# Down product of a decoder trunk's first row part in plain fp32, and a top-k search shared out anew between two engines

## What is computed

```python
# DSA: the 256 best-scoring keys of each query row, then attention over these
_, sel = lax.top_k(score, n_sel)
# MLP, D_FF = 2816 = 22 chunks of 128 columns
g_conv, new_ffn = causal_dwconv(ffn_buf, xn2 @ W['w_gate'][i], W['conv_ffn'][i])
h = h + (jax.nn.silu(g_conv) * (xn2 @ W['w_up'][i])) @ W['w_down'][i]
```

## Time and profile before

| what | us |
|---|---|
| median of three runs | 1925.38 |
| profiled execution, its own time | 1921.14 |
| its span | 1919.5 |
| PE busy in the span | 1699.0 |
| DVE busy | 1153.1 |
| ACT busy | 748.1 |

### The profile page before, as it was taken

The page is one execution under the profiler, slowest core; times in us unless marked ns, Lnnn a source line. Parts: engine busy times, 40 slices in busy tenths (PEclk is TensorE's granted clock), DMA queues, the critical chain, the costliest instruction groups (busy, mean ns, idle before and its releaser), DMA issues.

```text
span 1919.5 us, 27805 instructions
## 1 busy us (share of the span) xinstructions
PE 1699.0 (89%) x9909; PEld 1528.4 (80%) x9909; DVE 1153.1 (60%) x2454; ACT 748.1 (39%) x1349; POOL 211.3 (11%) x356
## 2 busy tenths in 40 slices
PE   6989998987768888778999998799999999998894
PEld 5978897863557666556888898799999999997793
DVE  5456764386767876688655554455555555554544
ACT  4343443353568477723444432232222222225321
POOL 1000000121101212222633100000000000000000
PEclk9999999998867777878999999899999999999996
DMA  5321121331312222232323223112121212231002
GB/s 182 108 99 55 56 86 65 110 117 47 99 39 90 83 78 77 86 110 67 108 90 96 75 68 124 55 55 78 66 77 66 76 66 76 66 104 45 22 34 90
DMA packets 50226, 153.19 MB, mean 80 GB/s; under 512 B 9456, under 2 KB 12528, under 8 KB 50112
## 3 DMA queue, kind: packets, MB, share of 16 engines
q1 hardware_dynamic: 35248, 116.13, 17.7%
q0 software_dynamic: 14864, 35.60, 5.9%
HBM read 141.92 MB, written 9.76 MB: 79 GB/s over the span
## 4 chain that ended last, share of the span: by engine, by line
PE 55%; issue 12%; DVE 9%; ACT 5%; DMA 1%; POOLq 1%; POOL 1%; DVEq 0%; ACTq 0%
PE ps L1874 20%; PE ps L735 14%; PE ps L1975 8%; ACT act_junk L1230 3%; PE ps L1356 2%; PE ps L1396 2%; PE ps L1410 2%; PE ps L2141 1%; PE ps L1368 1%; PE ps L1422 1%; PE ps L1050 1%; DVE Pb_b L1605 1%; DVE wl L521 1%; DVE junk_b L1174 1%; DVE SC L1082 1%
## 5 line engine op out<-in xcount | busy, mean ns | idle before, releaser
L521 DVE TENSOR_TENSOR wl<-wr,wh 128x1024 fp32r<-128x1024 f32 x202 | 246.7, 1223 | 295.6 <-ACT wh L514 294.2
L514 ACT ACTIVATE wh<-wr 128x1024 fp32r<-128x1024 f32 x202 | 213.0, 1056 | 456.2 <-PE ps L1874 196.0
L1874 PE MATMUL ps<-xh_b,wh 128*128 128x336 f32 x832 | 264.7, 318 | 8.7 <-DVE xl_b L619 4.9
L1874 PE MATMUL ps<-xl_b,wh 128*128 128x336 f32 x832 | 265.1, 319 | 0.0
L1874 PE MATMUL ps<-xh_b,wl 128*128 128x336 f32 x832 | 263.4, 317 | 0.0
L735 PE MATMUL ps<-xh_a,wh 128*128 128x384 f32 x592 | 219.9, 372 | 22.7 <-DVE xl_a L619 8.4
L735 PE MATMUL ps<-xh_a,wl 128*128 128x384 f32 x592 | 217.5, 367 | 0.0
L735 PE MATMUL ps<-xl_a,wh 128*128 128x384 f32 x592 | 214.7, 363 | 0.0
L1874 PEld LDWEIGHTS ps<-xh_b,wh 128*128 128x128 f32 x832 | 157.6, 189 | 10.5 <-DVE wl L521 4.1
L1874 PEld LDWEIGHTS ps<-xh_b,wl 128*128 128x128 f32 x832 | 157.6, 189 | 0.0
L1874 PEld LDWEIGHTS ps<-xl_b,wh 128*128 128x128 f32 x832 | 157.2, 189 | 0.0
(11 more groups left out here) (365 smaller groups left out, 3432.5 us busy)
## 6 DMA issues: line engine op xcount, KB each, us to landing
wr<-in_weights SPq DMA_DIRECT2D x202, 512.0 KB, 3.5
pages<-in_d_pages POOLq DMA_DIRECT2D x128, 128.0 KB, 2.4
out_y<-TN SPq DMA_DIRECT2D x8, 528.0 KB, 2.7
pages<-in_c_pages POOLq DMA_DIRECT2D x128, 32.0 KB, 2.1
H<-in_xT SPq DMA_DIRECT2D x8, 336.0 KB, 9.3
H<-in_xT POOLq DMA_DIRECT2D x8, 336.0 KB, 5.4
H<-in_xT SPq DMA_DIRECT2D x8, 192.0 KB, 5.5
H<-in_xT POOLq DMA_DIRECT2D x8, 192.0 KB, 4.5
```

The source lines that it names most:

```text
L514: nc.scalar.activation(wh[:, slot], wr[:, slot], ACT.Copy).then_inc(w_hi, 1)
L521: nc.vector.tensor_tensor(wl[:, slot], wr[:, slot], wh[:, slot].bitcast(f32), ALU.subtract).then_inc(w_lo, 1)
L1874: last = nc.tensor.matmul(bank(first_bank + c)[:, 0:CB], w, x, start=k == 0 and t == 0, stop=k == KC - 1 and t == 2)
```

## The change

Three things:

1. The first part's down product takes the raw weights `wr` and the undivided rows `gu_a` in plain fp32, with no split of either, over four chunks at a time (five groups of four and one of two). The weights are stored a second time in the order this needs (W_DA on); each such block holds 4 chunks for 2 of the 8 outputs. A group's four blocks are used one after each of the next four chunks. `gu_a` holds eight chunks. `half_conv` is made once for all chunks, and the two zero columns of `ge_a` are set once.
2. Each mask becomes two stages, `need` (count, comparison, how many equal ones to take) and `mask` (scan and the rest); the threshold gets a stage `found`, where the reload of the scores is now issued.
3. Array 2 (768 keys) of the search moves from ACT to DVE.

```diff
-ACT_TOP = [4, 3, 2, 1]
-DVE_TOP = [5, 0]
+ACT_TOP = [4, 3, 1]
+DVE_TOP = [5, 2, 0]
...
+def add_down(g, part):
+    left = min(4, FC - 4 * g)
+    rows = 8 // left
+    ORDER.append(W_DA + 4 * g + part if left == 4 else ff_block("d", 4 * g, part))
+    SKIPPED.append(len(ORDER) - 1)
+    QUANTA.extend(("d", g, rows * part + m, left, len(ORDER) - 1) for m in range(rows))
+for f in range(FC):
+    add_chunk(f)
+    if f >= 4:
+        left = min(4, FC - f // 4 * 4)
+        for part in range(f % 4 * 4 // left, (f % 4 + 1) * 4 // left):
+            add_down(f // 4 - 1, part)
+for part in range(2):
+    add_down(QUADS - 1, part)
...
+LENGTH = [{"d": 4 * NA, "pb": CB}.get(QUANTA[n][0], NA) for n, _ in MM]
...
-            + [("mask", NTOP - 1)] + [("mask", j) for j in range(NTOP - 1)])
+            + ["found"] + [(what, j) for j in [NTOP - 1, *range(NTOP - 1)] for what in ("need", "mask")])
-    weights = [{"sign": 4, "ties": 8, "mask": 8}.get(s[0] if type(s) is tuple else s, 4) for s in stages]
+    weights = [{"sign": 4, "ties": 8, "mask": 6, "found": 2}.get(s[0] if type(s) is tuple else s, 4) for s in stages]
...
             if j == 0:
-                pe.wait_ge(w_lo, s + 1)
+                if kind == "d":
+                    pe.wait_ge(w_raw[s % 3], 16 * (s // 3 + 1))
+                else:
+                    pe.wait_ge(w_lo, split_no(s) + 1)
...
                 if kind == "d":
-                    pe.wait_ge(a_lo, 2 * f + 2)
+                    pe.wait_ge(a_mul, 4 * f + count)
...
             if kind == "d":
                 cols = slice(0, NA)
-                w, x = three(t, s % 3, (ah_a[:, (2 * f + k) % 3], al_a[:, (2 * f + k) % 3]), 4 * k + c % 4)
+                rows = 8 // count
+                w, x = wr[:, s % 3, rows * j + c % rows], gate_up_a(4 * f + j)
...
-                nc.scalar.activation(ah_a[:, f % 3], gv_a[:, f % 2, 0:NA], ACT.Copy).then_inc(a_hi, 1)
...
-                nc.vector.tensor_tensor(al_a[:, f % 3], gv_a[:, f % 2, 0:NA], ah_a[:, f % 3].bitcast(f32), ALU.subtract).then_inc(a_lo, 1)
...
-            nc.vector.tensor_tensor(v, v, bank(6 + n % 2)[:, 0:NA], ALU.mult).then_inc(a_mul, 1)
+            nc.vector.tensor_tensor(gate_up_a(f), v, bank(6 + n % 2)[:, 0:NA], ALU.mult).then_inc(a_mul, 1)
...
-            nc.vector.memset(e[:, 0:2], 0.0)
-            link(nc.vector.tensor_scalar(w, p_("conv_ffn")[:, 3 * f:3 * f + 3], 0.5, None, ALU.mult))
...
-        SEARCHED_AT = [4 * n + p for (n, p), s in B_STAGE_AT.items() if s == ("mask", NTOP - 1)][0]
+        SEARCHED_AT = [4 * n + p for (n, p), s in B_STAGE_AT.items() if s == "found"][0]
```

More of the change, by code:

```diff
@@ L172, with spread @@
 assert 4 * (IDX_STEP + 6) == 4 * SIDX_STEP
-def spread(total, places):
-    weight = sum(w for _, w in places)
-    out, done = {}, 0
+def spread(first, last, places):
+    weight, total = sum(w for _, w in places), sum(LENGTH[first:last])
+    out, done, n, length = {}, 0, first, 0
     for place, w in places:
         done += w
-        out[place] = round(total * done / weight)
+        while n < last and length + LENGTH[n] / 2 <= total * done / weight:
+            length += LENGTH[n]
+            n += 1
+        out[place] = n
+    out[places[-1][0]] = last
     return out
 MM = [(n, j) for n, q in enumerate(QUANTA) for j in range(q[3]) if q[0] != "pa"]
+LENGTH = [{"d": 4 * NA, "pb": CB}.get(QUANTA[n][0], NA) for n, _ in MM]
 N_PB, N_OUT = 2 * NZ * 24, KC * 24
@@ L190 @@
 ISSUED = {}
[L191 to L194, removed]
+ISSUED |= spread(0, N_PB, [(p, 1) for p in range(0, 4 * PROJ_END)])
+ISSUED |= spread(N_PB, N_PB + N_OUT, [(p, 1) for p in range(4 * PROJ_END, NORM_AT - 4)])
+ISSUED |= spread(N_PB + N_OUT, len(MM), [(p, 1.0 if p < 4 * DSA_B else 1.2) for p in range(FFN_AT, NPOS)])
 for p in range(NPOS):
@@ L215, in limit @@
     return min([NPOS - 1] + [START[a] for a in (n,) if a in START])
-FREE_AT, HI_AT, LO_AT, CONV_AT, TANH_AT, MUL_AT, AH_AT, AL_AT = ({} for _ in range(8))
+FREE_AT, HI_AT, LO_AT, CONV_AT, TANH_AT, MUL_AT = ({} for _ in range(6))
 MUL_FIRST = {}
@@ L243 @@
         MUL_FIRST[f] = at > tanh_at
-        at = put(AH_AT, min(at + 1, limit(down)), f)
-        put(AL_AT, min(at + 1, limit(down)), f)
 for s in range(NZ + 2, NFIRST):
+    if s in SKIPPED:
+        continue
     first = limit(FIRST_Q[s])
@@ L700, in build, with split_no, gate_up_a @@
         LAST_A_UNIT = unit(A_END)
+        def split_no(s):
+            return s - sum(a < s for a in SKIPPED) if type(s) is int else s - len(SKIPPED)
+        def gate_up_a(f):
+            return gu_a[:, f % 8] if f % 8 < 6 else gu_rest_a[:, f % 8 - 6]
         def freed(n):
@@ L1253, in thresholds, with need @@
                 dve.wait_ge(self.searched, 1)
-            def mask(self, dve, link, j, back=None):
+            def need(self, dve, link, j, back=None):
                 at, S, rows = self.arrays[j]
-                sc, junk, equal, run = self.scores(j), self.junk[0:rows, 0:S], self.equal[0:rows, 0:S], self.run[0:rows, 0:S]
+                sc, equal = self.scores(j), self.equal[0:rows, 0:S]
                 if back:
@@ L1262, in mask @@
                 link(nc.vector.tensor_scalar(self.col(NEED, j, rows), self.col(CNT, j, rows), -1.0, float(TOPK), ALU.mult, ALU.add))
+            def mask(self, dve, link, j):
+                at, S, rows = self.arrays[j]
+                sc, junk, equal, run = self.scores(j), self.junk[0:rows, 0:S], self.equal[0:rows, 0:S], self.run[0:rows, 0:S]
                 link(nc.vector.tensor_tensor_scan(junk, run, equal, 0.0, ALU.mult, ALU.add))
@@ L2372, in weight_blocks @@
     out += [rows(w_ple_gate[:, m * P:(m + 1) * P]) for m in range(KC)]
+    for g in range(FC // 4):
+        w = w_down[4 * g * P:(4 * g + 4) * P].reshape(4, P, 4, 2, P)
+        out += [w[:, :, part].transpose(1, 0, 2, 3).reshape(P, KC, P) for part in range(4)]
     assert len(out) == NW
```

70 lines of the change are left out of this document (34 added, 36 removed).

## The result

1877.68 us, the median of four runs (1877.11 to 1881.75), against 1926.96 (1919.97 to 1930.78) for the kernel before, run beside it: ratio 0.9753, 95% interval [0.9721, 0.9785]. The prediction said 1910, between 1884 and 1937. The direction was right, the size was not: 49 us instead of 15, and the time lies under the range. The profiled execution took 1877.43 us, its span is 1875.8.

The account below looks back on a forecast made before the run. A chain changing engine bounds steps 42 to 66, TensorE the sparse attention. Terms 7 + 2 + 4 - 20 + 5 - 6 - 5 = -13 took 1921.1 to 1908, moved half way back to the median: 1910 us, range 1884 to 1937.

Parts of the forecast that it names:

- The plain product, 0.645 us: Down product on TensorE: each plain product costs 0.645 us against 0.525 before, +21.1 us for 176 at full clock.
- The rival of the weight loads: Down product: plain weights are not loaded in time and every record pays 0.104 us, giving 1940 us; chance 0.03.
- Sparse attention: +7: Sparse attention: +11.5 us of longer TensorE matmuls, less 4.5 us back from its stalls, leaves +7 us.
- About a third counts, +4: Steps 42 to 66: about a third of TensorE's extra 11 us for the plain product reaches the time, +4 us.
- the +2: Places 149 to 167, 19 of the first 119: TensorE's extra plain-product time costs +2 us.
- the clock comes back: Search and masks: fewer turns and more matmul time hold TensorE's clock at 0.85 in the search, 1895 us; chance 0.17.
- I take -20, between -8 and -26: Steps 42 to 66: VectorE loses splits and adds worth 26 us, of which 20 us come off the time.
- -5, between +5 and -10: Down product: 88 quanta become 48, so fewer turns between engines, set against a new wait, give -5 us.
- Net +5, between -12 and +17: Search, third array moved to VectorE: -12 us where VectorE waited, +17 us where it was late already, net +5 us.
- -6: Masks in two stages: half of TensorE's 22.7 us of waits go, and half of that reaches the end, -6 us.
- Nothing comes of it: Rival: relief and price nearly cancel as VectorE's idle time for logits grows by what it saves, 1921 to 1925; chance 0.19.
- TensorE pays: Rival, steps 42 to 66: all of TensorE's extra work counts and little VectorE relief comes through, 1941 us; chance 0.15.

Follow-up runs that it names:

- everything else undone: Changed kernel with pairs of chunks and the halves of weights and rows kept as instructions, leaving only the plain matmuls of the plain product: 1911.2 us.
- the repeat: The changed kernel profiled and measured once more, with nothing altered: 1877.3 us.
- the fourth pass on the changed kernel: Changed kernel with low rows by low weights added in the up product, 30.8 us more TensorE work: 1891.2 us.
- the fourth pass on the kernel before: Kernel before with low rows by low weights added in the down product, 30.8 us more TensorE work: 1951.6 us.
- the pages sooner: Changed kernel with the sparse attention's sample pages asked for up to five places sooner on GpSimd's queue: 1871.0 us.

## Why the prediction was wrong

Its sum was 13 in TensorE's part (7 + 2 + 4), -25 in relief and turns, -1 in array and masks. The runs give -3, -34 and -10 along one path (array and masks first, then the plain matmuls, then the rest); as the parts do not add up, another order gives other shares. Three steps failed: the turns, sized at 5 where they brought 12 to 16; TensorE's longer matmuls before the sparse attention, charged with +6 where search and masks got shorter; and the third array, +5 where it gave 13 to 16 beside the plain product.

- **The bound**: right. A chain that changes engine sets the search, and what shortens the turns shortens it.
- **The plain product, 0.645 us**: right, records 0.325 apart. The Trainium skill's page "FP8 and Floating Point Precision" (section "TensorE Precision Notes") says that true fp32 takes four passes of the array; the trace agrees, since 0.65 us are four times 384 columns at 2.4 GHz. The rival of the weight loads fell by the same number, and the rule cited for it, as I had applied it, does not hold here.
- **"Sparse attention: +7"**: the profile shows +7.3, and this is a coincidence. The price was right (+8.6 with everything else undone), but what comes back was not 4.5: the plain product alone ended at +0.8, as TensorE's idle time fell from 6.6 to 2.8 us and the clock rose from 0.97 to 0.99. The 6.5 above that came from the clock, which no term had: 20.4 us of the stretch ran at 1.2 GHz against 6.8 with the plain product alone. Half of the difference is the longer spell behind the late page, the other half are two later spells whose cause is open.
- **"About a third counts, +4"** and the +2: wrong in sign. Search and masks got 13.1 us shorter when only the matmuls were changed (one profile each), at a clock of 0.79 for 0.73. I priced TensorE's work at the clock that I had read, as if it were fixed. The clock moved as the rival "the clock comes back" said, which I had put beside the sum with 0.17: its value of 0.85 was met (0.86, in the repeat 0.83). Whether the clock caused the shorter search or came with it is open, since 259.0 and 258.1 us were taken at 0.86 and 0.83. Its 1895 was too high in any case, since it left the other terms as they were.
- **"I take -20, between -8 and -26"** and **"-5, between +5 and -10"**: together -25 for a measured -34. The relief was about right: the halves of weights and rows and the adds gave 5.1, 7.0 and 5.5 as single pieces, 17.6 for my 20, and 21.3 in search and masks alone. The turns gave 12 by the times and 16 by the stretches, outside my bounds. I had priced a turn by the waits at the down product alone and not by who waits behind it: VectorE's 19.4 us for the logits went to 1.4 as well.
- **"Net +5, between -12 and +17"**: measured -2 alone, which is no change, and -16 with the plain product (-13 with split masks too). The 17 us for stages in which VectorE was late anyway were counted at full length, on a VectorE that the other terms had just relieved; this is my reading, no run isolates it. VectorE's count takes 1.01 us, as estimated.
- **"-6" for the masks**: -6 without the plain product, nothing with it. The reload wait stayed, as said (3.00, then 3.7 us).
- **"Nothing comes of it"** and **"TensorE pays"**: fell. What VectorE was relieved of came through, and the plain matmuls' extra work outside the sparse attention cost nothing, nor did the fourth pass on the changed kernel. TensorE is not free there in general, as the fourth pass on the kernel before showed (+20.8 us in search and masks).

What would have shown it right: act_junk under 12 us (10.4), plain records 0.32 apart (0.325), the sparse attention 3 to 12 longer (7.3, for another reason), all met; search and masks 15 to 28 shorter was 43.6; TensorE's waits at dense matmuls under 25 us: 2.5.

## What to carry to other kernels

In a stretch where no engine is full, count the turns between engines that an edit removes, and look who waits behind each; here 40 turns were worth some 12 us in the time, and the halves of 22 weight blocks 5. Where the granted clock is well under 1, do not take TensorE's added work at that clock as the price: here it cost between nothing and most of its length, by what stood beside it, so add a pass and measure. Parts of a change that relieve and load the same engine do not add up, so try each with and without the others; and after a gain, look at the first transfer that is now late.

## What the runs showed of the hardware

A wait of 2.3 us for the sample pages was followed by 13.5 us at 1.2 GHz in one run of the changed kernel, and by some 7 in the kernel with the plain product alone (wait 2.3); one of 2.6 us was followed by none. In the first, the clock fell 1.8 us behind the wait, while TensorE ran the narrow products over the pages (weights 128x32 and 32x32); with the pages sooner the same products ran without a wait and the clock stayed at 1.00 for the next 20 us. The Trainium skill's page "TensorE: Matmul & The Clock Gate" (section "HAM oscillation — how this bites in real kernels") says that a transfer's wait throws the clock back; the trace agrees in kind, and shows that here it costs up to three times the wait or nothing. And with more work for TensorE alone the granted clock of the search stood at 0.80 instead of 0.73, in the same 293 us, on the kernel with array and masks. On the kernel before it went from 0.76 to 0.79 in the search and from 0.81 to 0.74 in the masks, so more work does not raise the clock everywhere.
